# A deferred norm in the feed-forward, modulations placed inside a bank, and latent norms in two steps, in a two-block network kernel

## The reference

```python
xn = rmsnorm(x, norm1_g)                      # x * rsqrt(mean(x*x) + eps) * g
proj = xn @ w_in                              # SSD, MLA and GDN inputs, gate logits
...                                           # three mixers: y_ssd, y_mla, y_gdn
mixed = g_ssd * (y_ssd @ w_ssd_out) + g_mla * (y_mla @ w_mla_out) + g_gdn * (y_gdn @ w_gdn_out)
h = x + mixed @ w_out
f = jnp.square(jax.nn.relu(rmsnorm(h, norm2_g) @ w_up)) @ w_down
return h + f
```

```python
sh1, sc1, g1, sh2, sc2, g2 = [m[:, None, :] for m in ada_mod(c, ada_w[i], ada_b[i])]
h_lat = rms_norm(x_lat, norm1_g[i]) * (1 + sc1) + sh1
h_ctx = rms_norm(x_ctx, norm1_g[i]) * (1 + csc1) + csh1
...
x_lat = x_lat + g1 * out_lat
x_lat = x_lat + g2 * swiglu(rms_norm(x_lat, norm2_g[i]) * (1 + sc2) + sh2, ffn_w_in[i], ffn_w_out[i])
```

## Time and profile before

| | |
|---|---|
| three runs | 2816.16 to 2820.49 us, median 2819.86 us |
| the profiled execution, its own time | 2831.51 us |
| its span in the trace | 2829.7 us |
| mean granted clock of TensorE in it | 0.967 |
| TensorE | busy 95% of the span, 20188 matmuls |
| VectorE, ScalarE, GpSimd | busy 54%, 45%, 14% |
| memory read | 380.25 MB, 135 GB/s over the span |
| a DMA of 1 MB of weights | 4.7 us from issue to landing (median for win) |

### The profile page before, as it was taken

One profiled execution on the slowest core, in us unless ns is written; L12 is line 12 of the kernel. 1 busy time (PEld: TensorE's weight loads), 2 busy tenths in 40 slices (PEclk: granted clock), 3 DMA queues, 4 the chain that ended last, 5 costly groups with the idle time before them and its releaser, 6 DMA issues.

```text
span 2829.7 us, 46160 instructions
## 1 busy us (share of the span) xinstructions
PE 2694.6 (95%) x20188; PEld 2484.6 (88%) x20188; DVE 1525.9 (54%) x2272; ACT 1261.6 (45%) x1887; POOL 387.1 (14%) x226
## 2 busy tenths in 40 slices
PE   7999999999999999999999999999999999998999
PEld 6989898799999998987999987578778999888999
DVE  3764467466446644674665524664333563766554
ACT  5724454455457234544554435653223452223442
POOL 4153100000042531000000001420000000331000
PEclk8999899899999998998999999999999999999999
DMA  4322334345543223343544323243333552112454
GB/s 158 132 93 89 119 135 164 119 164 181 190 142 131 105 90 120 135 164 119 179 173 170 134 105 134 96 159 119 131 126 131 196 195 99 69 52 92 162 183 175
DMA packets 56025, 384.27 MB, mean 136 GB/s; under 512 B 6032, under 2 KB 9744, under 8 KB 9872
## 3 DMA queue, kind: packets, MB, share of 16 engines
q1 hardware_dynamic: 55104, 376.14, 37.5%
q10 hardware_dynamic: 720, 5.18, 0.5%
HBM read 380.25 MB, written 1.05 MB: 135 GB/s over the span
## 4 chain that ended last, share of the span: by engine, by line
PE 77%; DVE 14%; ACT 6%; issue 1%; POOL 1%; DMA 1%; SPq 0%; DVEq 0%; POOLq 0%; ACTq 0%
PE ps L874 18%; PE ps L876 17%; PE ps L875 17%; DVE r L2011 4%; ACT r L1413 2%; PE ps L835 2%; PE ps L1355 1%; PE ps L989 1%; PE ps L947 1%; PE ps L945 1%; PE ps L946 1%; PE ps L1074 1%; PE ps L1066 1%; PE ps L910 1%; PE ps L1079 1%
## 5 line engine op out<-in xcount | busy, mean ns | idle before, releaser
L874 PE MATMUL ps<-r,r 128*128 128x256 f32 (+1 forms) x4512 | 1357.2, 301 | 33.8 <-DVE r L2011 31.7
L875 PE MATMUL ps<-r,r 128*128 128x256 f32 (+1 forms) x4512 | 1342.0, 297 | 0.0
L876 PE MATMUL ps<-r,r 128*128 128x256 f32 (+1 forms) x4512 | 1341.6, 297 | 0.0
L2011 DVE TENSOR_TENSOR r<-ring,r 128x1024 fp32r<-128x1024 f32 (+2 forms) x558 | 681.6, 1256 | 513.8 <-ACT r L1413 513.6
L874 PEld LDWEIGHTS ps<-r,r 128*128 128x128 f32 x4512 | 865.5, 192 | 65.3 <-DVE r L2011 20.7
L875 PEld LDWEIGHTS ps<-r,r 128*128 128x128 f32 x4512 | 865.2, 192 | 24.0 <-issue 0.5
L876 PEld LDWEIGHTS ps<-r,r 128*128 128x128 f32 x4512 | 864.2, 192 | 24.9
L1413 ACT ACTIVATE r<-ring 128x1024 fp32r<-128x1024 f32 (+1 forms) x614 | 613.6, 1038 | 283.3 <-DMA ring<-in_fi 66.3
L2833 POOL TENSOR_TENSOR slab<-slab 128x512 f32<-128x512 f32 (+1 forms) x20 | 28.1, 1407 | 1399.8 <-ACT slab L1539 1375.7
L2791 POOL TENSOR_TENSOR r<-ring,r 128x1024 fp32r<-128x1024 f32 x56 | 132.1, 2385 | 185.4 <-ACT r L1413 185.2
L2088 DVE SCALAR_TENSOR_TENSOR slab<-ps,v,slab 128x255 f32<-128x255 f32 (+1 forms) x168 | 67.4, 472 | 96.8 <-ACT slab L1493 96.7
(11 more groups left out here) (320 smaller groups left out, 3180.6 us busy)
## 6 DMA issues: line engine op xcount, KB each, us to landing
ring<-in_win SPq DMA_DIRECT2D x76, 1024.0 KB, 4.7
ring<-in_ada SPq DMA_DIRECT2D x48, 1024.0 KB, 4.7
ring<-in_fi SPq DMA_DIRECT2D x44, 1024.0 KB, 4.8
ring<-in_fo SPq DMA_DIRECT2D x36, 1024.0 KB, 4.7
ring<-in_wup SPq DMA_DIRECT2D x32, 1024.0 KB, 4.8
ring<-in_wdn SPq DMA_DIRECT2D x32, 1024.0 KB, 4.8
ring<-in_hin SPq DMA_DIRECT2D x20, 1024.0 KB, 4.7
ring<-in_nqkv SPq DMA_DIRECT2D x12, 1024.0 KB, 4.7
```

Source lines behind the costliest of these rows:

```text
L874: self.mm(o, hi[:, k - k0, cs], xh, k == 0, False)
L875: self.mm(o, hi[:, k - k0, cs], xl, False, False)
L876: i = self.mm(o, lo[:, k - k0, cs], xh, False, k == last)
L2011: self.tt(K.low(p), K.raw(p), K.high(p).bitcast(F32), ALU.subtract).then_inc(*self.up("w_lo_v", p))
```

## The change

It touches five places.

1. norm2. The input of wup becomes `split(x * gain)`, made pair by pair between wo's banks in a new stream `deferred`; the factor of each token (the root) is applied at the eviction of wup, where `relu2` now is one VectorE instruction from PSUM, `max(P, 0) * rs`, and two squares on ScalarE, one giving the high part and one the value in place. The low part of a bank is made one bank later. The squares' sum stands at the end of wup's lead (`sums`). The factor lies in `K.gate[:, 0, :]`. The table for the root is loaded ahead of the last square of wo and wdn.
2. wo, wup, wdn, gz, `no` and `fo` of case 1, and hq become fine. `context` and `mod` stand between a bank's weights and its eviction, and are cut at tiles 3, 6 and 8.
3. The latent norms become two steps, kn and then qn, with a half bank of gz between them each time.
4. Among MLA's fills an ada0 group and a gate_m bank change places, and the ada0 group of the last step but one moves with them.
5. The order of layer 1 begins with an ada0 group, which is taken from those behind wup.

```diff
-        n1, n2, J = xk(("n1", L)), xk(("n2", L)), {}
+        n1, n2, J = xk(("n1", L)), lambda k: ("n_v", ("lo", ("n2", L), k)), {}
...
-        win("gz", 36, 44, "act", dst=self.z2, func=ACT.Silu, free=lambda g: [("gd_v", ("y", L, 6))])
+        win("gz", 36, 44, "act", dst=self.z2, func=ACT.Silu, fine=True, free=lambda g: [("gd_v", ("y", L, 6))])
...
-        J["wo"] = Job(("wo", L), "wo", L, range(8), T, self.ms, mk, "onto_x", power=("n2", L))
-        J["wup"] = Job(("wup", L), "wup", L, range(32), T, self.xn, n2, "relu2", hid=self.hid, lead=2)
+        J["wo"] = Job(("wo", L), "wo", L, range(8), T, self.ms, mk, "onto_x", power=("n2", L), fine=True)
+        J["wup"] = Job(("wup", L), "wup", L, range(32), T, self.xn, n2, "relu2", hid=self.hid, lead=2, sums=("n2", L), fine=True)
...
-        J["wdn"] = Job(("wdn", L), "wdn", L, range(8), T, self.hid, hk, "onto_x", power=("n1", L + 1))
+        J["wdn"] = Job(("wdn", L), "wdn", L, range(8), T, self.hid, hk, "onto_x", power=("n1", L + 1), fine=True)
...
-                J["no", case] = Job(("no", case), mat, 0, range(8), T, self.h_of[case], ok, "onto", goff=16, layer2=0, case=case, power=("m2", M, case))
+                J["no", case] = Job(("no", case), mat, 0, range(8), T, self.h_of[case], ok, "onto", goff=16, layer2=0, case=case, power=("m2", M, case), fine=case == 1)
...
+    if L:
+        yield ("ada0", 1)
...
-    yield from [("ssd", 1), ("gz", 1), ("ssd", 1), ("gz", 1), ("ssd", 1), ("gz", 1), ("mla", 1), ("ssd", 1), ("gz", 1), ("wuk", 1), ("ssd", 1),
+    yield from [("ssd", 1), ("gz", 2), ("ssd", 1), ("gz", 2), ("ssd", 1), ("gz", 1), ("mla", 1), ("gz", 1), ("ssd", 1), ("gz", 1), ("mla", 1),
+                ("gz", 1), ("wuk", 1), ("ssd", 1),
...
-    for fill in ("wso", "wso", "gate_m", "ada0", "gate_m", "ada0", "gate_m", ("split wmo", "ada0"), "ada0", "split wmo"):
+    for fill in ("wso", "wso", "gate_m", "ada0", "gate_m", "ada0", "ada0", "gate_m", ("split wmo", "ada0"), "split wmo"):
...
-    yield from [("wso", None), ("gate_m", None), ("wmo", None), ("wo", None), ("norm2", None)]
+    yield from [("wso", None), ("gate_m", None), ("wmo", None), ("wo", 3)]
+    for _ in range(2):
+        yield from [("norm2", 1), ("wo", 2)]
+    yield from [("norm2", 1), ("wo", None), ("norm2", 1), ("wup", 1), ("norm2", None)]
...
     for _ in range(3):
-        yield from [("wup", 2), ("context", 1)]
+        yield from [("wup", 4), ("context", 1)]
     yield from [("wup", None), ("ada0", None), ("wdn", 1), (("scales", 0), None)]
     for _ in range(3):
-        yield from [("context", 1), ("wdn", 1)]
+        yield from [("context", 1), ("wdn", 2)]
...
+        yield (("no", 1), 1)
         for _ in range(3):
-            yield from [(("no", 1), 1), (mod(0, 2, 0), 1)]
+            yield from [(mod(0, 2, 0), 1), (("no", 1), 2)]
+        yield (mod(0, 2, 0), None)
...
-    yield from [("hq", 1), (mod(1, 1, 1), 1), ("hq", 1), (mod(1, 1, 1), 1), ("hq", 1), (mod(1, 1, 1), None), ("hq", None),
+    yield from [("hq", 1), (mod(1, 1, 1), 1), ("hq", 2), (mod(1, 1, 1), 1), ("hq", 2), (mod(1, 1, 1), 1), ("hq", 2), (mod(1, 1, 1), None), ("hq", None),
...
@@ TensorE.dense, end of a bank; end of lead
-                if pid and i0 == 8:
+                if pid and i0 == 8 and pid[0] != "n2":
                     self.power_own(pid)
...
+        if "sums" in job.more and not halves:
+            self.power_own(job.more["sums"])
+            self.power_sum(job.more["sums"], 6)
...
@@ ScalarE.squared, relu2, root, deferred; mla
+            if i == 6 and pid[0] in ("n1", "n2"):
+                self.e.preload_act_table_set(LN_EXP)
...
-        self.act(f, P, ACT.Relu).then_inc(*self.up("ev_s", "relu", job.key, g))
-        self.emptied("ev_s", "d", job.key, g)
-        self.wait_ge(*self.at("ev_v", "square", job.key, g))
-        self.act(job.more["hid"][0][:, g:g + 2, :], f, ACT.Copy).then_inc(*self.up("ev_s", "hi", job.key, g))
+        f, hi = self.K.tmp[g // 2 % 3], job.more["hid"][0][:, g:g + 2, :]
+        self.wait_ge(*self.at("ev_v", "relu", job.key, g))
+        self.act(hi, f, ACT.Square).then_inc(*self.up("ev_s", "hi", job.key, g))
+        self.act(f, f, ACT.Square).then_inc(*self.up("ev_s", "square", job.key, g))
...
-        self.e.preload_act_table_set(LN_EXP)
+        if pid[0] not in ("n1", "n2") or pid == ("n1", 0):
+            self.e.preload_act_table_set(LN_EXP)
...
+    def deferred(self, pid):
+
+        K, gain = self.K, self.K.V1[pid[1]][pid[0]]
+        for i in range(0, 8, 2):
+            self.wait_ge(*self.at("ev_v", "x", ("wo", pid[1]), i))
+            for j in range(i, i + 2):
+                self.act(K.xn[0][:, j, :], K.x[:, j, :], ACT.Copy, scale=gain[:, j:j + 1]).then_inc(*self.up("n_s", "hi", pid, j))
+            yield
+        self.root(pid, K.gate[:, 0, :], T, 1 / 1024)
         yield
...
         self.highs(kn, K.square_of(kn), K.kn, 2)
+        yield
         self.highs(qn, K.square_of(qn), K.qn, 4)
...
-        yield from self.shifted(pid, l, 24 * (which - 1), (4, 8))
+        yield from self.shifted(pid, l, 24 * (which - 1), (3, 6, 8))
...
@@ VectorE.relu2, deferred
+        self.wait_ge(*self.at("dense_p", job.key, g))
+        self.wait_ge(*self.at("n_s", "rs", job.more["sums"]))
+        self.stt(f, P, 0.0, bc(self.K.gate[:, 0:1, :], [128, 2, T]), ALU.max, ALU.mult).then_inc(*self.up("ev_v", "relu", job.key, g))
+        self.emptied("ev_v", "d", job.key, g)
+        for i in (g - 2,) if g < job.last() else (g - 2, g):
+            if i >= 0:
+                hi, lo = (v[:, i:i + 2, :] for v in job.more["hid"][:2])
+                self.wait_ge(*self.at("ev_s", "square", job.key, i))
+                self.tt(lo, self.K.tmp[i // 2 % 3], hi.bitcast(F32), ALU.subtract).then_inc(*self.up("ev_v", "lo", job.key, i // 2))
...
+    def deferred(self, pid):
+        K, gain = self.K, self.K.V1[pid[1]][pid[0]]
+        for i in range(0, 8, 2):
+            for j in range(i, i + 2):
+                self.wait_ge(*self.at("n_s", "hi", pid, j))
+                self.stt(K.xn[1][:, j, :], K.x[:, j, :], gain[:, j:j + 1], K.xn[0][:, j, :].bitcast(F32), ALU.mult, ALU.subtract).then_inc(*self.up("n_v", "lo", pid, j))
+            yield
         yield
```

More of the change, by code:

```diff
@@ L530, in jobs_block2 @@
             for case, mat in enumerate(("fo", "fo_c")):
-                J["fo", case] = Job(("fo", M, case), mat, 0, range(8), T, self.hid_of[case], hk, "onto", goff=40, layer2=0, case=case, power=("m1", 3, case))
+                J["fo", case] = Job(("fo", M, case), mat, 0, range(8), T, self.hid_of[case], hk, "onto", goff=40, layer2=0, case=case, power=("m1", 3, case), fine=case == 1)
         else:
-            J["hq"] = Job(("hq", M), "hin", 0, range(8), T, self.h_of[0], xk(1, 0), "act", dst=self.hq, func=ACT.Silu)
+            J["hq"] = Job(("hq", M), "hin", 0, range(8), T, self.h_of[0], xk(1, 0), "act", dst=self.hq, func=ACT.Silu, fine=True)
             J["hv"] = Job(("hv", M), "hin", 0, range(8, 16), 512, h, xk(1, 1), "rows", to=[self.hvt[:, m, :] for m in range(4)])
@@ L603, in order2 @@
         yield from [(("fi", 0), None), (("scales", 1), None), (("fo", 0), None)]
+        yield (("fo", 1), 1)
         for _ in range(3):
-            yield from [(("fo", 1), 1), (mod(1, 1, 0), 1)]
+            yield from [(mod(1, 1, 0), 1), (("fo", 1), 2)]
+        yield (mod(1, 1, 0), None)
         yield (("fo", 1), None)
         return
-    yield from [("hq", 1), (mod(1, 1, 1), 1), ("hq", 1), (mod(1, 1, 1), 1), ("hq", 1), (mod(1, 1, 1), None), ("hq", None),
+    yield from [("hq", 1), (mod(1, 1, 1), 1), ("hq", 2), (mod(1, 1, 1), 1), ("hq", 2), (mod(1, 1, 1), 1), ("hq", 2), (mod(1, 1, 1), None), ("hq", None),
                 ("bounds", None), ("hv", None), (("hf", 0, 0), None)]
@@ L715, in program @@
             self.streams |= {"norm1": self.norm(("n1", L), L == 0), "angles": self.angles(), "small": self.small(L), "qk": self.qk(L),
-                             "gdn": self.gdn(L), "ssd": self.ssd(L), "mla": self.mla(L), "norm2": self.norm(("n2", L), False)}
+                             "gdn": self.gdn(L), "ssd": self.ssd(L), "mla": self.mla(L), "norm2": self.deferred(("n2", L))}
             self.follow(order1(L))
@@ L735, in norm @@
     def norm(self, pid, own):
+        yield from ()
+    def deferred(self, pid):
         yield from ()
@@ L862, in dense @@
                         self.lead(job, lead)
+                    if job.parts() == 2:
+                        yield
                     continue
@@ L2135, in relu2 @@
         f = self.K.tmp[g // 2 % 3]
-        hi, lo = (v[:, g:g + 2, :] for v in job.more["hid"])
-        self.wait_ge(*self.at("ev_s", "relu", job.key, g))
-        self.tt(f, f, f, ALU.mult).then_inc(*self.up("ev_v", "square", job.key, g))
-        self.wait_ge(*self.mine("ev_v"))
-        self.wait_ge(*self.at("ev_s", "hi", job.key, g))
-        self.tt(lo, f, hi.bitcast(F32), ALU.subtract).then_inc(*self.up("ev_v", "lo", job.key, g // 2))
```

(4 more changed lines are left out.)

8 lines of the change are left out of this document (4 added, 4 removed).

## The result

The changed kernel took 2777.29 us in the median of four runs (2774.44 to 2783.14), against 2819.77 before (2816.16 to 2820.49): a ratio of 0.9855, 95% interval 0.9837 to 0.9873. A second set of four, timed beside eleven runs of the kernel before, gave 2785.63 (2782.85 to 2788.16) against 2820.97: ratio 0.9873, interval 0.9856 to 0.9890. The forecast was 2774, range 2756 to 2800. So both sets lie in the range, and both gains (42 and 35 us) are smaller than the 45.7 forecast. The two medians of this one program lie 8.3 us apart, while those of the kernel before lie within 1.2.

A forecast was written before the change was run, and what follows sets the result against it. TensorE, busy 95% of 2829.7 us, bounds the kernel; edits gain only where it idles or runs at half clock. Terms sum to 45.7 us: profiled 2831.5 becomes 2785.8, and 11.65 lower for the median, 2774; range 2756 to 2800.

The forecast's parts named there:

- norm2: Feed-forward norm ahead of wup's lead: shorter pauses and leads at full clock, gain 11.2 us, bounds 0 and 14.3.
- The new eviction: wup's fused VectorE instruction, taken as 0.69 us: nothing gained or lost, 0.36 us in hand per bank.
- slower rival: wup's fused eviction is slow, deciding above 2.48 us; 32 banks late, time 2813 or 2828; chance 0.04.
- Latents: Latent norms in two steps: 3.0 us of idle and 1.8 of clock saved per layer, 9.6, bounds 0 and 9.6.
- MLA: MLA's tail: wait for division cut from 5.94 to 0.4, 11.1 us; clock 2.6; sum 13.7, bounds 5.5 and 22.7.
- stalls' rival: VectorE full mid-bank, next bank's lows late: 19 us of context, MLA and latents not gained; 2793; chance 0.20.
- Context: Modulation steps moved mid-bank remove waits for weights: 2.3 us in wup, 6.85 in wdn.
- fo: Modulations moved mid-bank in fo: waits of 2.9 us should go, gain 2.85.
- no: Gap of 2.3 goes, but modulation steps push fi's lead 1.6 us later; bounds −5 and +2.3.
- hq: Of a 1.9 us wait before hv little goes; table loads fall from three to one or two; gain 0.6.
- norm1: Layer 1's first norm: ada group brings 1.6 us, lead goes 1.4 back; gain 0.2, bounds −1.4 and +3.0.
- The clock comes back whole: Where idle goes, clock dips go: MLA 9.0 and norm1's lead 2.5, 11.5 us more; 2763; chance 0.14.

The follow-up runs named there:

- undone: Each part of the change separately put back as before, starting from the changed kernel; for example norm2 2796.36 us, Latents 2787.73 us.
- the second trace: Profile of the changed kernel run once more with no edit; that set's median was 2785.63 us.
- the reference: The changed kernel's eight unedited runs, median 2783.0 us.
- MLA's old fills: Changed kernel with the fills of before among MLA's steps put back; 2788.59 us.

## Why the prediction was right, and where its terms were off

**norm2** (11.2): right, 11.1 by the traces and 12.5 undone. The lead took 5.86 and 5.89 us where 5.69 was put, and the sums 1.46 where 1.3 was; the 0.5 taken off layer 1 was roughly the difference seen (5.7 and 5.4). The reason stands on an experiment: the last pair of x did not bind, and with the sums back ahead of the lead nearly half the gain went. That layer 1's weights are ready later, the reason given for the 0.5, was not tried. The upper bound of 14.3 takes the six matmuls as gone as well; with them kept it is 11.8.

**The new eviction** (0): right, and for the reason given. The instruction takes 691 ns where 0.69 was taken from the earlier trace rows; banks are 5.69 us apart. The margin per bank is 0.56 instead of 0.36. The slower rival would have needed an instruction of (0.56 + 0.69) + 45.7/32 = 2.68 us.

**Latents** (9.6): right, 9.4, the 3.0 us and 1.7 of clock in each layer.

**MLA** (13.7): the term that was mis-sized, 8.6 and 6.8 in the two traces. Of its two parts the idle is the one that failed clearly: 11.1 was forecast, and by the lists of waits it fell from 13.6 to 7.2 (6.3 and the new 0.9), so 6.4, and in the second trace 7.0. That leaves 2.2 and −0.2 for the clock, where 2.6 was put. "I leave 0.4" was for the old place only: the two ada0 groups now stand behind one another, and the division that ends the new wait (525.90) lies behind the lows of the second group's weights (523.37) on VectorE, just as the old one lay behind lows. That is the stalls' rival, one link later, in one place: 2.0 us in each layer. A fourth bank of gate_m there takes the wait away and gives the lowest median of the study, 2775.50. And the 2.6 of clock is a draw: between two executions of one program MLA's two layers differed by 5.1 and 3.3 us, in opposite directions.

**Context** (9.15): right, 9.6. The prediction had weighed up to 5.1 us of slower weight lows beside GpSimd against this part, and took none, since the lows would come first. None was lost, but not because they never meet: in wdn four lows, the first two beside GpSimd's sums, took 7.16 us, and four without took 4.72, while TensorE waited for nothing from 1350 to 1620 us.

```profile
1529.45 7.16 DVE L2043 TENSOR_TENSOR r<-ring,r 128x1024 fp32r<-128x1024 f32 x4 [2.45 <-ACT r L1434]
```

**fo** (2.85): 3.7. **no** (−1.6): −1.3 and −0.3; the wait that ended it was not the lows, as argued, but GpSimd's sum of squares. With whole banks the lows bind again and the time is no better, so the forecast loss from the place is not shown. **hq** (0.6): mis-sized, 2.8 by the traces and 1.3 undone. I had left 1.7 of its 1.85 us; what was left of the wait is 0.17 and 0.5. **norm1** (0.2): 0.7 and −0.2, but not for the reason given; the idle fell from 4.0 to 3.5, and it is 3.5 without the group as well. What shortened it stays open.

**The total.** Terms as measured add up to 44.6 and 42.9, against 45.7; with 3.8 and 3.1 from places that the change does not touch, the two traces gain 48.4 and 46.1. That this is near 45.7 is in part luck: MLA lacks 5.1 and 6.9, and hq (2.2 over), the smaller terms and the untouched places make up for it. The medians gain 42 and 35. The weak step is the last one of the sum, a gain read against one execution and then taken off the median unchanged: that execution of before was 11.65 us longer than the median, at a mean clock of 0.967 against 0.969 to 0.974 in 33 later runs of the same kernel. The changed kernel's first profiled execution lay 5.9 above its median, the second at it. norm2, the latents and the context lost as much or more when undone from the side of the changed kernel, clock included, so they are not where it lies; it can lie in MLA or in places without an edit. Which, stays open: there is one trace of before, and the column "undone", which does not use it, adds up to 44.6 and 43.9 too. Medians don't settle it either: that of the kernel with `no` undone lies 1.4 below the reference, those with one of the other parts undone 5 to 15 us above, some by less and some by more than their stages lost. One more slip is in the forecast's own range: the bounds of norm2 and MLA do give 2762 below, but 2793 above, not 2788.

Of the rivals, none held as a whole. "The clock comes back whole" was true of norm2, the latents and wdn, and false of MLA: there the dip stayed with 2.0 us of idle before it, and was gone (1.00) or nearly (0.97) in the two traces in which a bank stood there. The Trainium skill ("TensorE: Matmul & The Clock Gate", Part 1) ties the clock to how busy the array has been; the prediction had set a dip without idle before it against that, and the trace with the extra bank agrees with the page rather than with me: full clock over both layers' light steps, once a bank of 48 matmuls stood between two of them. My own row does not speak against the page as I took it to: ahead of the 2.82 us at half clock TensorE had executed nothing but light work for 8.94 us, 54 small matmuls at full clock. The kernel without the ada0 group, with the same fills, was granted 0.97 in both layers, so the page's rule gives the direction here and not the whole of it.

## What to carry to other kernels

A norm's factor that is constant along the contracted axis can be taken at the output, and with it the sums leave the path as well; check then the engine that takes over the eviction, by its own loop over a bank and not by one bank's chain. When light work is used as a filler, look for two light fillers in a row: here the second one's preparation delayed what the first was to hide, and the clock fell there as well. And clock losses read from one execution are a draw; carry them to a median only after a second trace.

## What the runs showed of the hardware

The same program, with waits equal to a tenth, was granted 0.97 and 0.87 over MLA's two layers in one execution and 0.87 and 0.92 in the next, which moved each layer by 3 to 5 us. Over the runs of one kernel the time goes with the mean clock: before, in one set, 2813.9 us at 0.973 and 2825.3 at 0.970, in another 2813.5 at 0.974 and 2828.8 at 0.969.

A second, smaller effect does not show in the granted clock. A bank of 48 in the last feed-forward lasts 5.60 us in 11 of the 14 traces, 5.65 in two (the first of the changed kernel is one) and 5.76 in one, MLA's old fills: 2.9% more than 5.60, at a granted clock of 1.00 and with TensorE never idle. The windows of the same 60 us, of the kernel before and of that experiment:

```profile
2700.00:2760.00 60.00, 60.00 (x517) 1.00 0.54 188
```
```profile
2700.00:2760.00 60.00, 60.00 (x503) 1.00 0.55 193
```

Banks of 48 lasted 5.60 us in the one and 5.76 in the other (by these windows, 60 us x 48 / 517 and / 503: 5.57 and 5.73). Against the second trace of the changed kernel, with 5.60 too, that is 5.2 us over the stage. The last edited step lies some 1.3 ms ahead of that stage, and what sets the length of a bank was not tried.
